# A two-layer decoder trunk with grouped experts: gathered rows of the second expert in a place of their own, two ScalarE steps and one table in another order, and expert weights loaded as 16 KB rows

## The reference

```python
h = layer_norm(ALPHA * h + mix, ln_g[layer, 0], ln_b[layer, 0])
ffn = grouped_moe(h, router_w, router_bias, w_gate[layer], w_up[layer], w_down[layer])
h = layer_norm(ALPHA * h + ffn, ln_g[layer, 1], ln_b[layer, 1])
```

## Time and profile before

| | us |
|---|---|
| median of 3 runs (1215.83 to 1216.56) | 1215.86 |
| the profiled execution: its own time | 1215.64 |
| the profiled execution: span from first to last instruction | 1213.9 |
| PE busy in it | 1179.1 |
| DVE busy in it | 899.7 |
| ACT busy in it | 704.3 |

### The profile page before, as it was taken

The page is one execution under the profiler, slowest core; times in us unless marked ns, Lnnn a source line. Parts: engine busy times, 40 slices in busy tenths (PEclk is TensorE's granted clock), DMA queues, the critical chain, the costliest instruction groups (busy, mean ns, idle before and its releaser), DMA issues.

```text
span 1213.9 us, 14999 instructions
## 1 busy us (share of the span) xinstructions
PE 1179.1 (97%) x5770; PEld 933.1 (77%) x5771; DVE 899.7 (74%) x1196; ACT 704.3 (58%) x867; POOL 181.9 (15%) x152
## 2 busy tenths in 40 slices
PE   7999999999999999999999999999999999999995
PEld 5787588887888887876787776768888888888873
DVE  5275555779998989989644455675789899899886
ACT  4432524257786776875334453573367877778772
POOL 1000010112131221210000000000112222222111
PEclk9999999999999999999999999999999999999998
DMA  8223031259999999998230420322379999999973
GB/s 289 72 74 135 1 104 70 87 207 415 366 372 376 371 374 366 355 367 303 70 105 19 156 87 18 109 89 81 115 300 399 374 368 365 382 372 364 372 270 138
DMA packets 65947, 280.95 MB, mean 231 GB/s; under 512 B 12592, under 2 KB 12848, under 8 KB 41298
## 3 DMA queue, kind: packets, MB, share of 16 engines
q1 hardware_dynamic: 49248, 247.55, 53.3%
q0 software_dynamic: 12000, 27.85, 8.0%
q10 hardware_dynamic: 4626, 4.57, 1.2%
HBM read 269.93 MB, written 25.20 MB: 243 GB/s over the span
## 4 chain that ended last, share of the span: by engine, by line
PE 78%; DMA 10%; DVE 7%; ACT 2%; issue 2%; POOL 0%; DVEq 0%; SPq 0%; POOLq 0%; ACTq 0%
PE ps L718 21%; PE ps L720 21%; PE ps L719 21%; DMA ring<-in_moe_w_up_dram 7%; DVE ring_r L1629 3%; PE ps L1177 2%; PE ps L1187 2%; PE ps L902 2%; PE ps L1200 2%; DMA ring<-in_moe_w_down_dram 1%; PE ps L911 1%; DMA ring<-in_kv_w_dram 1%; PE ps L799 1%; PE ps L1116 1%; PE ps L1104 1%
## 5 line engine op out<-in xcount | busy, mean ns | idle before, releaser
L1629 DVE TENSOR_TENSOR ring_r<-ring,ring_r 128x2048 fp32r<-128x2048 f32 x128 | 291.9, 2286 | 8.0 <-ACT ring_r L1367 7.8
L1367 ACT CAST ring_r<-ring 128x2048 fp32r<-128x2048 f32 x128 | 242.8, 1926 | 18.0 <-DMA ring<-in_moe_w_gate_dram 9.6
L719 PE MATMUL ps<-ring_r,xgT_r 128*128 128x512 f32 x528 | 206.0, 390 | 0.0
L1367 ACT CAST high_r<-ring 128x2048 fp32r<-128x2048 f32 x64 | 122.2, 1912 | 122.1 <-DMA ring<-in_moe_w_up_dram 117.8
L1629 DVE TENSOR_TENSOR ring_r<-ring,high_r 128x2048 fp32r<-128x2048 f32 x64 | 146.1, 2291 | 37.1 <-ACT high_r L1367 36.9
L614 POOL DMA_INDIRECT sum_rows<-arena,tokv x28 | 57.3, 2048 | 390.6 <-ACT arena L1418 390.6
L719 PEld LDWEIGHTS ps<-ring_r,xgT_r 128*128 128x128 f32 x528 | 99.4, 188 | 18.6
L718 PE MATMUL ps<-ring_r,xgT_r 128*128 128x512 f32 x272 | 108.9, 400 | 0.0
L720 PE MATMUL ps<-ring_r,xgT_r 128*128 128x512 f32 x272 | 106.2, 390 | 0.0
L718 PE MATMUL ps<-featT,ring_r 128*128 128x512 f32 x256 | 103.8, 406 | 0.0
L718 PE MATMUL ps<-high_r,xgT_r 128*128 128x512 f32 x256 | 102.3, 400 | 0.2
(11 more groups left out here) (278 smaller groups left out, 2088.8 us busy)
## 6 DMA issues: line engine op xcount, KB each, us to landing
ring<-in_moe_w_gate_dram SPq DMA_DIRECT2D x64, 1024.0 KB, 12.3
ring<-in_moe_w_up_dram SPq DMA_DIRECT2D x64, 1024.0 KB, 13.4
ring<-in_moe_w_down_dram SPq DMA_DIRECT2D x64, 1024.0 KB, 13.2
ring<-in_gla_w_in_dram SPq DMA_DIRECT2D x6, 2048.0 KB, 10.0
ring<-in_kv_w_dram SPq DMA_DIRECT2D x4, 2048.0 KB, 12.8
ring<-in_fox_w_qg_dram SPq DMA_DIRECT2D x4, 2048.0 KB, 8.2
ring<-in_gla_w_out_dram SPq DMA_DIRECT2D x2, 2048.0 KB, 8.5
h_rows<-arena POOLq DMA_DIRECT2D x8, 512.0 KB, 2.9
```

What stands on the lines that cost most here:

```text
L719: pe.matmul(o, left[0], right[1], start=False, stop=False)
L1367: act.copy(high, w).then_inc(half_high, 1)
L1629: dve.tensor_tensor(low, w, high.bitcast(F32), ALU.subtract).then_inc(half_low, 1)
```

## The change

There are three parts.

- The gathered rows of expert 1 go to `turned[:, 5:7, :]`, and their gather is issued when all rows are stored and the table of expert 1 is there. It no longer waits for `h_scaled` and `xt_done`. Expert 2 keeps its place and its waits.
- ScalarE does the exponential and the two copies into `info` ahead of the high part of half 2. The scaling of the last tile moves from before the Silu to behind `take_rows(0)`. TensorE does the table of expert 3 before the transposes of the hidden values of expert 0, not behind them.
- From half 8 on SP issues one DMA for each even n. It waits until half n - 7 is used, and brings both halves, 2 MB, as 128 rows of 16 KB. ScalarE waits for it once, at the even half.

```diff
@@ -233,6 +233,11 @@
         f_log, f_tmp = at(3072, S)[0:H_B, :], at(3584, S)[0:H_B, :]
 
         xg = at(2048, 2, D)
+        second_rows = turned[:, 5:7, :].rearrange("p a n -> p (a n)")
+
+        def rows_at(e):
+            return second_rows if e == 1 else xg[:, e % 2, :]
+
         Hp = at(2048, T, D)
         hid, silu = at(4096, BANK), at(4608, BANK)
         hidT, high_arena, xgT = hidT_r[:, :, :], high_r[:, :, :], xgT_r[:, :, :, :]
@@ -506,12 +511,18 @@
                             sp.wait_ge(last_rows_stored, 32 * (L + 1))
                         if n == 6:
                             sp.wait_ge(gathered[1], 16 * (8 * L + 1))
+                    elif h:
+                        continue
                     else:
-                        sp.wait_ge(half_used, half_count(L, n - RAW_HALVES))
+                        sp.wait_ge(half_used, half_count(L, n + 1 - RAW_HALVES))
                     slot, c = half_slot(L, n)
                     w = {"gate": moe_w_gate, "up": moe_w_up, "down": moe_w_down}[kind]
                     src = w[L, e].rearrange("(q k) f -> q k f", q=P)
                     ks = src.shape[1] // 2
+                    if n >= RAW_HALVES:
+                        sp.dma_start(ring[:, slot, :].rearrange("p (k f) -> p k f", k=2 * ks), src
+                                     ).then_inc(half_loaded[n % RAW_HALVES], 16)
+                        continue
                     sp.dma_start(ring[:, slot, c].rearrange("p (k f) -> p k f", k=ks),
                                  src[:, h * ks:(h + 1) * ks, :]).then_inc(half_loaded[n % RAW_HALVES], 16)
 
@@ -619,12 +630,13 @@
                 if L == 0:
                     pool.dma_start(dummy[0:1, :], x[0, 0:1, 0:P]).then_inc(c_sca, 16)
                 pool.wait_ge(first_rows_stored, 32 * (L + 1))
+                pool.wait_ge(last_rows_stored, 32 * (L + 1))
+                pool.wait_ge(tbl_ev, 2 * E * L + 1)
+                gather(rows_at(1), tokv[:, 1, 0:1], gathered[1])
                 pool.wait_ge(h_scaled, T * L + 2)
-                pool.wait_ge(last_rows_stored, 32 * (L + 1))
                 pool.wait_ge(xt_done, 2 * (E * L + 1))
-                for n, e in enumerate(ENTRY[:2]):
-                    pool.wait_ge(tbl_ev, 2 * (E * L + n) + 1)
-                    gather(xg[:, e % 2, :], tokv[:, e, 0:1], gathered[e % 2])
+                pool.wait_ge(tbl_ev, 2 * E * L + 3)
+                gather(rows_at(2), tokv[:, 2, 0:1], gathered[0])
                 for e in range(E + 1):
                     if 1 <= e <= SCATTERED:
                         pool.wait_ge(y_ev, 2 * (E * L + e))
@@ -889,6 +901,11 @@
                                        start=s == 0, stop=s == T - 1)
                     return mm
 
+                def next_table(e):
+                    pe.wait_ge(hot, E * L + e + 1)
+                    pe.wait_ge(tbl_ev, 2 * (E * L + e))
+                    table(e, onehot[:, e % 2, :]).then_inc(tbl_done, 1)
+
                 def entry_table(e):
                     pe.wait_ge(hot, E * L + e + 1)
                     for s in range(T):
@@ -956,7 +973,7 @@
                         entry_table(ENTRY[2])
                     if e + 1 < E:
                         pe.wait_ge(gathered[(e + 1) % 2], 16 * ((7 + (e + 1) % 2) * L + e // 2 + 1))
-                        turn_rows(xg[:, (e + 1) % 2, :], xt_done)
+                        turn_rows(rows_at(e + 1), xt_done)
                     if e < E:
                         if e >= 1:
                             pe.wait_ge(hid_done, E * L + e)
@@ -972,13 +989,13 @@
                             down(e - 1, (1,))
                         else:
                             down(e - 1)
+                    if e == 0:
+                        next_table(3)
                     if e < E - 1:
                         pe.wait_ge(hid_done, E * L + e + 1)
                         turn_hidden(hid).then_inc(ht_done, 1)
-                    if e + 3 < E:
-                        pe.wait_ge(hot, E * L + e + 4)
-                        pe.wait_ge(tbl_ev, 2 * (E * L + e + 3))
-                        table(e + 3, onehot[:, (e + 3) % 2, :]).then_inc(tbl_done, 1)
+                    if 0 < e < E - 3:
+                        next_table(e + 3)
 
                 pe.wait_ge(counted, L + 1)
                 most = pe.value_load(counts[0:1, E:E + 1], min_val=0, max_val=S)
@@ -1344,21 +1361,23 @@
                 take_normed(L)
 
             def router(L):
-                high_half(L, 2)
                 act.wait_ge(rt_in, 2 * (L + 1))
                 act.activation(rt[1][:, EARLY:T, :], rt[0][:, EARLY:T, :], ACT.Exp).then_inc(rt_exp, 1)
                 for m in range(2):
                     act.copy(info[:, :, 0:E, m], row_id[:, :].unsqueeze(2).to_broadcast([P, T, E])
                              ).then_inc(rt_info, 1)
+                high_half(L, 2)
                 high_half(L, 3)
-                scale_residual(L, T - 1)
                 own.mark(act.activation(ln_r[:, 0, 2:3], half[:, 0:1], ACT.Silu))
                 act.wait_ge(rt_ranks, 2 * (L + 1))
                 act.copy(total[:, :], ps[0:1, 5, 0:E]).then_inc(rt_total, 1)
 
             def high_half(L, n):
 
-                act.wait_ge(half_loaded[n % RAW_HALVES], 16 * (HALVES // RAW_HALVES * L + n // RAW_HALVES + 1))
+                if n % 2 == 0:
+                    act.wait_ge(half_loaded[n % RAW_HALVES], 16 * (HALVES // RAW_HALVES * L + n // RAW_HALVES + 1))
+                elif n < RAW_HALVES:
+                    act.wait_ge(half_loaded[n % RAW_HALVES], 16 * (L + 1))
                 if n >= HIGH_HALVES:
                     act.wait_ge(half_used, half_count(L, n - HIGH_HALVES))
                 elif n >= 2:
@@ -1377,6 +1396,7 @@
                         act.copy(xgT[:, e % 2, 0, kk * BANK:(kk + 1) * BANK], ps[:, kk, :]).then_inc(xt_high, 1)
 
                 take_rows(0)
+                scale_residual(L, T - 1)
                 high_half(L, 4)
                 high_half(L, 5)
                 begin_sums(L, T - 1)
```

## The result

The changed kernel takes 1220.98 us at the median of five runs (1217.35 to 1223.12), the kernel before 1215.83 beside it. The ratio is 1.0037, 95% interval 1.0021 to 1.0052. By the ratio it is 4.5 us slower, where 4.3 us less were forecast. The profiled execution took 1220.09 us, its span 1218.3.

A forecast was written before the change was run, and what follows sets the result against it. It took the DMA weight stream to decide late in each layer, TensorE before. Layer 0 gains 2.4 us, layer 1 1.7 plus 0.2 from the router, together -4.3: 1211.6 us, range 1207 to 1219.5.

The forecast's parts named there:

- entry: gather, exponential, table: Layer start: earlier gather nets 1.3 us a layer, exponential 0.2 us in layer 1; the table only gives TensorE lead.
- issue of a slot's halves together, when both are used: SP's weight queue: issuing a pair some 3 us later is hidden by queueing in the late stretch, cost nothing.
- seen whole: second low part, end of layer 1: Behind a pair's landing, ScalarE and VectorE do both halves: 2.3 us later in layer 0, 3.2 at layer 1's end.
- rows of 16 KB for two of 8 KB: Weight stream: one 16 KB row takes 11.5 ns less than two of 8 KB, 0.28 us less an expert.
- So issuing 3 us later costs nothing there.: Late stretch: a half takes 16.2 us from issue to landing, mostly queue, 2.5 us its own bytes, so lateness is free.
- The loop needs them some 30 us after their issue: Gathers in the expert loop: 12.2 us flight leaves ample time; only expert 2's rows are needed sooner.
- 2.4 us more per gather: Gathered rows each wait behind 16 KB instead of 8; sum unchanged, or 0.5 us worse a layer if expert 2's come late.
- TensorE's floor: Layer 0 can end at most 4.4 us earlier before TensorE decides; a rival, chance 0.19, had it reached, 1207.8 us.
- 18.8 speaks for the second rival: Up-pair landings still 18.8 us apart would mean a 16 KB row costs as two of 8: 1218.6 us, chance 0.20.
- A fixed cost for each transfer: Weight transfers: 2.0 us a DMA plus bytes would save 2 us per merged pair; rejected as contradicting the queued trace.
- The third, a stream that runs dry: Pairs issued late begin late, 0.5 us for the first 12, 6 us a layer: 1223.6 us, chance 0.18.
- a DMA share below 0.95 in the first 40 us: After up 1's issue, the profile sign that the weight stream runs dry; otherwise the share would be near 1.

The follow-up runs named there:

- parts12: The changed kernel with each half again its own 8 KB-row transfer, issued as early as before, all other edits kept: 1211.15 us, 0.9960 of the kernel before.
- two_8k_own: The changed kernel with each 16 KB-row transfer split into two of 8 KB rows, issued together equally late, ScalarE waiting for each half: 1223.76 us, 1.0056.
- two_8k_both: `two_8k_own` with ScalarE waiting for both halves before it casts the first: 1227.88 us, 1.0099 of the kernel before.
- late_all: `parts12` with every half, odd ones too, waiting for the use of one half more than it needs: 1216.69 us, 1.0014 of the kernel before.
- after_tail: The changed kernel with the last three slots of each layer (up 15, down 14, down 15) going half by half again: 1221.66 us, 1.0051.
- after_early: The changed kernel with expert e+3's table ahead of the down products and its gather issued ahead of the scatter: 1221.86 us, 1.0048 of the kernel before.
- light_fine: `parts12` with scatters adding the rows of 16 of 128 partitions only, the other sums left out: 1203.34 us, 0.9896 of the kernel before.
- parts_early: `parts12` with expert e+3's table ahead of the down products and its gather ahead of the scatter: 1209.72 us, 0.9941 of the kernel before.
- place_only: The kernel before with only the second expert's gathered rows in their own place and their gather ahead: 1211.78 us, 0.9962.
- late_up: `parts12` with each expert's first up half issued together with the second, 8 KB rows and a semaphore each: 1213.31 us, 0.9979 of the kernel before.

## Why the prediction was wrong

The range, 1207 to 1219.5, lies below the median. The terms of the sum can now be set beside runs that differ in one thing each. Percent are of 1216 us, and a difference of two ratios is good to some 0.2%, 2.4 us.

| step | forecast us | from | measured us |
|---|---|---|---|
| entry: gather, exponential, table | -2.8 | before to `parts12` | -4.9 |
| issue of a slot's halves together, when both are used | 0 | `parts12` to `two_8k_own` | +11.7 |
| seen whole: second low part, end of layer 1 | +5.5 | `two_8k_own` to `two_8k_both` | +5.2 |
| rows of 16 KB for two of 8 KB | -7.0 | `two_8k_both` to after | -7.5 |
| sum | -4.3 | | +4.5 |

**The step that failed** is "So issuing 3 us later costs nothing there." It put the term at 0; it measured 11.7 us. With 0 there the other measured terms add up to -7.2, so this one is the whole miss. The reason given was a queue of 16.2 us at its median, against 2.5 us of own bytes. The queue is that long, and `late_all` shows that the reason holds in part for halves issued one by one: their flight shrinks by 3.0 us, and the loss is 0.54%. It doesn't hold where two halves are issued at once: the late ones of `two_8k_own` fly 12.8 us for 13.1, and the loss is 0.96%. A time from issue to landing is one figure for a whole transfer; it doesn't say that none of the engines runs short of work in between.

**The other terms.** Rows of 16 KB came out as forecast. The entry gained more, 4.9 us (interval 2.9 to 6.8) for 2.8. For the whole landing 5.2 stands beside 5.5, but that it arises where the prediction put it is not shown: 3.2 of the 5.5 were to lie at the end of layer 1, and `after_tail`, which goes half by half at both ends, got nothing back.

**Gathers.** "The loop needs them some 30 us after their issue" was wrong. In the trace of before the gather for expert 11 is issued 15.3 us before TensorE turns its rows, against a flight of 12.4:

```profile
433.37 2.40 POOL L608 DMA_INDIRECT arena<-h_rows,tokv  x1 [0.30 <-issue]
```

```profile
448.62 1.04 PE L902 MATMUL ps<-ident,arena 128*128 128x128 f32 x8
```
The Trainium skill ("DMA: Bandwidth & Descriptors", "Queues, rings and completion order") has each engine take turns between queues packet by packet, from which 2.4 us more per gather were worked out, with one weight row taken for one packet. The flight went from 12.4 to 17.2 us in 320:520, and the wait appeared in 19 places. `two_8k_both`, which differs from the changed kernel in the length of the rows alone, has 12.7 us there, so the row's length does it: in the direction of the rule, and by twice its arithmetic. No run shows the turns themselves. The wait had no price that `after_early` could win back: that step of the prediction was wrong and harmless.

**The bound** was read rightly: light scatters alone give 0.64% (`parts12` to `light_fine`), TensorE then is busy throughout the late stretch, and DMA falls from 8% to 0% of the chain. The room down to TensorE's floor was put too small. From the first gate product to the end of the last down product of layer 0 it is 296.35 us before and 290.06 in `light_fine`: 6.3 us of room, where the prediction had 4.4.

**Rate.** "18.8 speaks for the second rival" misled: the landings are 18.87 us apart not because long rows gain nothing, but since their gain and the late issue's loss cancel. Only kernels that part the two could tell.

**A fixed cost for each transfer.** The prediction set a fit of 2.0 us a DMA plus its bytes beside its sum. In the Trainium skill ("DMA: Bandwidth & Descriptors") that fit stands in the section "Anatomy of one DMA — SWDGE (gpsimd) path", not in "Bandwidth", and is for transfers that GpSimd issues. Here SP issues them, and one transfer in place of two gained 7.5 us over 88 pairs (`two_8k_both` to after), 0.09 us a pair and not 2.0.

**Rivals.** The third, a stream that runs dry, had the right sign, and its 6 us a layer stand beside the 5.9 of the late issue. Its place, the first pairs, was right too for the changed kernel as it stands. `parts12`, then the changed kernel:

```profile
286.00:306.00 20.00, 20.00 (x102) 16.79 (x102) 20.00 (x16) 15.93 (x15) 10.53 (x3) 1.00 0.99 391
```

```profile
286.00:306.00 20.00, 20.00 (x102) 16.83 (x101) 18.57 (x14) 15.69 (x14) 6.91 (x3) 1.00 0.98 353
```

The stream brings 353 GB/s for 391 there, a larger gap than in any window above, and `two_8k_own` has 348. VectorE starts the hidden values of expert 0 at the same time in `parts12` and the changed kernel (279.12 and 279.05), those of expert 6 at 385.58 and 388.40, and those of expert 15 at 551.30 and 553.97. So in these two executions the net loss of layer 0 against `parts12` is made in the first six steps, and behind them the two keep pace. `two_8k_own`, with short rows, is 1.9 us behind `parts12` at expert 6 and 5.9 at expert 15: the late issue goes on costing, and in the changed kernel the long rows pay for that. How much of the first 2.8 us is the late issue and how much the whole landing was not told apart. The sign that the prediction named for this rival, a DMA share below 0.95 in the first 40 us, would have missed it: the share is 0.98 at 353 GB/s.

**What stays open.** The size of the late issue's cost is shown, its mechanism is not. Open are why a late issue at gate or down costs so much and at up so little; why lateness of every half, spread evenly, costs about half of what pairs of issues cost; and why idle share and loss don't go together. A guess is that the 16 engines are far apart: in `two_8k_own` the gate halves issued at 464.80 and 465.23 landed 12.8 and 15.9 us later, though 2 MB are 5.7 us at 370 GB/s, and in 474:476 the share was 0.81 while they were still under way. Engines that are ahead would then idle without harm, and those behind would not. The traces as read here don't tell which engine a packet used, so this was not tested.

## What to carry to other kernels

When a transfer is issued once for two pieces of a buffer, price the later issue by an experiment with the old row length: halves that were 13.7 us in flight gave no slack for an issue some 3 us later. Longer rows did pay here, 7.5 us in all (0.30 us for each of the 25 experts that the prediction counted), and the earlier start did as well; the version to keep is `parts_early`, 0.6% under the kernel before, with each half issued as soon as it can be.

Before giving a wait a price, look for what sets the pace: removing 18.6 us of waits for gathered rows, the largest new item of the chain, gained nothing in a full stream, and taking 0.17 MB an expert off the queues gained 0.64%.

## What the runs showed that was not expected

TensorE's clock. In the entry of layer 0 four of the twenty profiled executions lose 1.5 us for a reason that is in none of the edits. `parts12`:

```profile
251.00:254.00 3.00, 2.91 (x13) 2.71 (x13) 2.66 (x4) 1.18 (x2) 0.47 (x2) 0.53 1.02 429
```

`place_only`:

```profile
251.00:254.00 3.00, 3.00 (x27) 2.79 (x25) 2.34 (x3) 2.18 (x3) 0.47 (x1) 1.00 1.01 423
```

The granted clock is 0.53 of full, so it stood at its lower level, 1.2 GHz, for nearly all of these 3 us, and 13 matmuls are done for 27. It fell in the profiled execution of the changed kernel, of `parts12`, of `two_8k_own` and of `late_up`, and not in that of before. In the 2 us ahead of it (249:251) TensorE was busy for 1.95 us in `parts12` and for 1.93 in before, with the same products in the same order, so what it did there doesn't tell the two apart. Starts of the first gate product compared between single executions (264.58 before, 266.10 after) hold this 1.5 us, and the medians of several runs are needed.
